# Experts in plain float32: weights stationary in two column tiles for gate and up, tokens in four for down

## The reference

```python
def swiglu(h, wg, wu, wd):
    g = jnp.einsum('btd,df->btf', h, wg)
    u = jnp.einsum('btd,df->btf', h, wu)
    return jnp.einsum('btf,fd->btd', jax.nn.silu(g) * u, wd)

def moe(h, router, wg, wu, wd):
    logits = jnp.einsum('btd,de->bte', h, router).astype(jnp.float32)
    vals, idx = lax.top_k(logits, TOP_K)
    gates = jax.nn.softmax(vals, axis=-1)
    comb = jnp.sum(jax.nn.one_hot(idx, N_EXPERTS, dtype=jnp.float32) * gates[..., None], axis=-2)
    out = jnp.zeros_like(h)
    for e in range(N_EXPERTS):
        out = out + comb[..., e:e + 1].astype(h.dtype) * swiglu(h, wg[e], wu[e], wd[e])
    return out
```

## Time and profile before

| what | value |
|---|---|
| median of 3 runs | 1280.8 us (1280.49 to 1281.12) |
| span of the profiled execution, first to last instruction | 1280.1 us |
| TensorE busy | 1262.4 us (99%), 6937 matmuls |
| VectorE, ScalarE busy | 934.3 us (73%), 803.0 us (63%) |
| HBM read | 340.57 MB, 273 GB/s over the span |
| granted clock of TensorE, mean | 0.999 |

### The profile page before, as it was taken

How to read it: one execution, slowest core, us unless ns; L and a number is a source line. 1 busy time by engine, 2 the same in 40 slices (tenths; PEclk the granted TensorE clock), 3 DMA queues, 4 the chain that set the end, 5 groups by cost and what they waited for, 6 DMA issues and landing times.

```text
span 1280.1 us, 18558 instructions
## 1 busy us (share of the span) xinstructions
PE 1262.4 (99%) x6937; PEld 1026.7 (80%) x6937; DVE 934.3 (73%) x888; ACT 803.0 (63%) x813; POOL 159.1 (12%) x175
## 2 busy tenths in 40 slices
PE   7999999999999999999999999999999999999998
PEld 5476699999974656788888888888888888888886
DVE  1667544443425667888888988988988988988897
ACT  2566533333324655767867877867867867777674
POOL 4131000000001020100310300400400400300300
PEclk9999999999999999999999999999999999999999
DMA  8261375445050624999999999999999999999994
GB/s 288 42 168 34 113 250 166 164 148 181 9 186 1 133 93 160 338 359 365 376 392 356 392 386 356 394 377 374 381 382 371 385 381 357 394 374 371 387 389 170
DMA packets 124595, 350.24 MB, mean 274 GB/s; under 512 B 8401, under 2 KB 33841, under 8 KB 124545
## 3 DMA queue, kind: packets, MB, share of 16 engines
q1 hardware_dynamic: 118896, 335.55, 71.9%
q0 software_dynamic: 4096, 12.43, 3.3%
q10 hardware_dynamic: 1552, 1.56, 0.4%
HBM read 340.57 MB, written 8.95 MB: 273 GB/s over the span
## 4 chain that ended last, share of the span: by engine, by line
PE 93%; DVE 3%; DMA 2%; ACT 1%; SPq 1%; issue 0%; DVEq 0%; ACTq 0%
PE ps L2337 38%; PE ps L2357 18%; PE ps L2244 11%; PE ps L1988 8%; PE ps L2260 5%; DMA ring<-in_w_in 2%; PE ps L2345 2%; PE ps L2061 1%; PE ps L2069 1%; PE ps L2121 1%; PE ps L2136 1%; PE ps L2174 1%; PE ps L2184 1%; PE ps L2001 1%; PE ps L2416 1%; PE ps L2085 1%
## 5 line engine op out<-in xcount | busy, mean ns | idle before, releaser
L1324 DVE TENSOR_TENSOR w_lo<-ring,w_hi 128x2048 fp32r<-128x2048 f32 (+1 forms) x322 | 675.2, 2124 | 178.8 <-ACT w_hi L938 176.4
L938 ACT ACTIVATE w_hi<-ring 128x2048 fp32r<-128x2048 f32 (+1 forms) x322 | 567.3, 1781 | 212.0 <-PE ps L2357 63.3
L2337 PE MATMUL ps<-w_hi,xg_hi 128*128 128x512 f32 (+1 forms) x768 | 287.8, 375 | 0.0
L2337 PE MATMUL ps<-w_hi,xg_lo 128*128 128x512 f32 (+1 forms) x768 | 286.1, 373 | 0.0
L2337 PE MATMUL ps<-w_lo,xg_hi 128*128 128x512 f32 (+1 forms) x768 | 285.4, 372 | 0.0
L2337 PEld LDWEIGHTS ps<-w_hi,xg_hi 128*128 128x128 f32 x768 | 144.6, 188 | 25.7
L2337 PEld LDWEIGHTS ps<-w_lo,xg_hi 128*128 128x128 f32 x768 | 144.2, 188 | 25.8
L2337 PEld LDWEIGHTS ps<-w_hi,xg_lo 128*128 128x128 f32 x768 | 144.6, 188 | 24.9
L2357 PE MATMUL ps<-w_hi,am_hi 128*128 128x512 f32 x340 | 133.7, 393 | 0.0
L2357 PE MATMUL ps<-w_lo,am_hi 128*128 128x512 f32 x340 | 132.5, 390 | 0.0
L2357 PE MATMUL ps<-w_hi,am_lo 128*128 128x512 f32 x340 | 132.3, 389 | 0.0
(11 more groups left out here) (357 smaller groups left out, 1435.2 us busy)
## 6 DMA issues: line engine op xcount, KB each, us to landing
ring<-in_moe_w_down SPq DMA_DIRECT2D x80, 1024.0 KB, 8.1
ring<-in_moe_w_gate SPq DMA_DIRECT2D x64, 1024.0 KB, 9.1
ring<-in_moe_w_up SPq DMA_DIRECT2D x64, 1024.0 KB, 9.4
ring<-in_moe_w_gate SPq DMA_DIRECT2D x32, 768.0 KB, 7.5
ring<-in_moe_w_up SPq DMA_DIRECT2D x32, 768.0 KB, 5.2
ring<-in_ffn_w_gate SPq DMA_DIRECT2D x11, 1024.0 KB, 7.4
ring<-in_ffn_w_up SPq DMA_DIRECT2D x11, 1024.0 KB, 5.3
ring<-in_ffn_w_down SPq DMA_DIRECT2D x10, 1024.0 KB, 5.2
```

The costliest lines, as they stand in the source:

```text
L938: A(hi[:, 0:size], src[:, 0:size], ACT.Copy).then_inc(hi_ready, 1)
L1324: V.tensor_tensor(lo[:, 0:size], src[:, 0:size], hi[:, 0:size].bitcast(F32), ALU.subtract).then_inc(lo_ready, 1)
L2337: ins = mm_(ps[:, b + c0 // 512, 0:c1 - c0], (xg_hi, xg_lo)[xp][:, k, :], w[wp][:, k % 2, c0:c1], start=(k == 0 and n == 0), stop=(k == KD ...
```

## The change

The experts leave float32r and the two parts. Weights are read as plain float32 from where the DMA put them.

- An expert has 96 places (`SLOTS`), three times 32.
- Gate and up: 64 columns of the weight are stationary, and the 96 tokens of `xg` move. Two column tiles take the two halves of a 128-column block, so the result stands with D_FF on the partitions, as down needs it; the transposes of `turn_chunk` and the split into `am_hi` and `am_lo` go.
- Down: the 96 tokens stand as three column tiles of 32 which move the first 768 columns of the weight; the fourth tile takes, one after another, the same three groups of tokens for the last 256 columns (`D_TAIL`). Their results stand on partitions 96 to 127 and are moved by ScalarE (`y_tail`).
- The ring of weights has twelve slots (`MOE_RING`): six in `ring`, six (`ring_more`) where `w_hi` and `w_lo` stood. A slot is free when TensorE has used it (`unit_used`).
- Gather of the first expert: both parts of a row accumulate in one bank and are turned once.
- Waits: up of chunk c + 1 waits for `act_done` of chunk c, `turn_rows` for `table_out`; at the head of the expert part `xh` waits for `stored`.

```diff
-SLOTS = P
+GRAN = DEC
+MAIN = P // GRAN - 1
+SLOTS = MAIN * GRAN
...
+BLOCKS = [w // P for w in WIDTH]
+HALF = P // 2
+D_TAIL = D // (MAIN + 1)
+D_LANE = D - D_TAIL
...
-DENSE_PAIRS, MOE_PAIRS = 3, 4
+DENSE_PAIRS = 3
+MOE_RING = 12
...
-        w_hi = [at(f"w_hi{i}", PHASE + 2 * SLOT_W * i, [P, SLOT_W], F32R) for i in range(MOE_PAIRS)]
-        w_lo = [at(f"w_lo{i}", PHASE + 2 * SLOT_W * i + SLOT_W, [P, SLOT_W], F32R) for i in range(MOE_PAIRS)]
+        w_hi = [at(f"w_hi{i}", PHASE + 2 * SLOT_W * i, [P, SLOT_W], F32R) for i in range(DENSE_PAIRS)]
+        w_lo = [at(f"w_lo{i}", PHASE + 2 * SLOT_W * i + SLOT_W, [P, SLOT_W], F32R) for i in range(DENSE_PAIRS)]
+        ring_more = [at(f"ring_more{i}", PHASE + SLOT_W * i, [P, SLOT_W]) for i in range(MOE_RING - RING)]
...
+        def unit_at(u):
+
+            i = u % MOE_RING
+            return ring[:, (MOE_AT + i) % RING, :] if i < RING else ring_more[i - RING][:, :]
...
-                sp.dma_start(ring[:, s, 0:n * wd].rearrange("p (n w) -> p n w", n=n), src).then_inc(w_ready[s], 16)
-
-            for u in range(RING):
-                slot_room(last_in_slot[(MOE_AT + u) % RING])
+                sp.dma_start(unit_at(u)[:, 0:n * wd].rearrange("p (n w) -> p n w", n=n), src).then_inc(unit_in[u % MOE_RING], 16)
+
+            for u in range(MOE_RING):
+                if u < RING:
+                    slot_room(last_in_slot[(MOE_AT + u) % RING])
+                elif u == RING:
+                    wait_full(sp, ("o", 1, len(GROUPS) - 1))
+                    sp.wait_ge(stored, 16 * DEPTH * 10)
                 load_unit(u, 0)
 
             def load_expert(j, e, first=0):
 
                 for u in range(first, len(EXPERT)):
-                    sp.wait_ge(lo_ready, j * len(EXPERT) + (ND + u - RING + 1))
+                    sp.wait_ge(unit_used, j * len(EXPERT) + (u - MOE_RING + 1))
...
-                    A(sgm[:, 0:WIDTH[c]], wide(0)[:, 0:WIDTH[c]], ACT.Silu).then_inc(silu_done, 1)
-
-                def chunk_high(c):
-                    w = WIDTH[c] // P
-                    act.wait_ge(aT_full, j * CHUNKS + (c + 1))
-                    A(am_hi[:, c % 2, 0:w, :], wide(4)[:, 0:w * P].rearrange("p (k c) -> p k c", k=w), ACT.Copy).then_inc(aT_high, 1)
+                    A(sgm[:, 0:BLOCKS[c], :], blocks(0, c), ACT.Silu).then_inc(silu_done, 1)
 
                 def output():
+
                     act.wait_ge(row_moved, j + 1)
-                    act.wait_ge(y_full, j + 1)
-                    A(y_out[:, :], wide(6), ACT.Copy, scale=slot_gate[:, 0:1]).then_inc(y_taken, 1)
+                    act.wait_ge(unit_used, j * len(EXPERT) + len(EXPERT))
+                    for g in range(MAIN):
+                        ins = A(y_out[GRAN * g:GRAN * g + GRAN, D_LANE:D], wide(6)[SLOTS:P, D_TAIL * g:D_TAIL * g + D_TAIL], ACT.Copy)
+                    ins.then_inc(y_tail, 1)
+                    A(y_out[0:SLOTS, 0:D_LANE], wide(6)[0:SLOTS, 0:D_LANE], ACT.Copy, scale=slot_gate[0:SLOTS, 0:1])
+                    act.wait_ge(y_tail, j + 1)
+                    A(y_out[0:SLOTS, D_LANE:D], y_out[0:SLOTS, D_LANE:D], ACT.Copy, scale=slot_gate[0:SLOTS, 0:1]).then_inc(y_taken, 1)
...
+                    V.tensor_tensor(am[:, c % 2, 0:BLOCKS[c], :], sgm[:, 0:BLOCKS[c], :], blocks(2, c), ALU.mult).then_inc(act_done, 1)
+
+                if not final:
+                    picks(bass.ds(j + 1, 1))
+                activations(0)
+                if not final:
+                    dve.wait_ge(row_moved, j + 1)
+                    table(j + 2)
+                activations(1)
+                activations(2)
+                if not final:
+                    dve.wait_ge(xgT_full, j + 2)
+                    tokens_second_half(5)
...
+                def lanes(b, x, w, main, tail, first, last):
+
+                    for c0 in range(0, main, 512):
+                        c1 = min(c0 + 512, main)
+                        for g in range(MAIN):
+                            ins = mm_(ps[GRAN * g:GRAN * g + GRAN, b + c0 // 512, 0:c1 - c0], x[:, GRAN * g:GRAN * g + GRAN], w[:, c0:c1],
+                                      start=first, stop=last)
+                        for g in range(MAIN):
+                            at_ = tail * g
+                            if c0 <= at_ < c1:
+                                ins = mm_(ps[SLOTS:P, b + c0 // 512, at_ - c0:at_ - c0 + tail], x[:, GRAN * g:GRAN * g + GRAN],
+                                          w[:, main:main + tail], start=(first and at_ == c0),
+                                          stop=(last and (g == MAIN - 1 or at_ + tail >= c1)))
+                    return ins
 
                 def project(kind, c, h):
+
                     u, wd = unit[kind, c, h], WIDTH[c]
+                    wait_unit(u)
+                    w = unit_at(u)[:, 0:2 * wd].rearrange("p (k c) -> p k c", k=2)
                     b = 0 if kind == "gate" else 2
-                    wait_unit(u)
-                    w = [x[u % MOE_PAIRS][:, 0:2 * wd].rearrange("p (k c) -> p k c", k=2) for x in (w_hi, w_lo)]
                     for k in (2 * h, 2 * h + 1):
-                        for c0 in range(0, wd, 512):
-                            c1 = min(c0 + 512, wd)
-                            for n, (wp, xp) in enumerate(PARTS):
-                                ins = mm_(ps[:, b + c0 // 512, 0:c1 - c0], (xg_hi, xg_lo)[xp][:, k, :], w[wp][:, k % 2, c0:c1],
-                                          start=(k == 0 and n == 0), stop=(k == KD - 1 and n == 2))
-                    in_use(ins, u)
-
-                def turn_chunk(c):
+                        for n in range(BLOCKS[c]):
+                            for half in range(2):
+                                c0 = P * n + HALF * half
+                                ins = mm_(ps[HALF * half:HALF * half + HALF, b + n // 4, P * (n % 4):P * (n % 4) + SLOTS], w[:, k % 2, c0:c0 + HALF],
+                                          xg[:, k, :], start=(k == 0 and n % 4 == 0), stop=(k == KD - 1 and n in (3, BLOCKS[c] - 1)))
+                    ins.then_inc(unit_used, 1)
...
+                        ins = lanes(6, am[:, c % 2, k0 + k, :], w[:, k, :], D_LANE, D_TAIL, c == 0 and h == 0 and k == 0, u == len(EXPERT) - 1 and k == n - 1)
+                    ins.then_inc(unit_used, 1)
...
-                project("gate", 1, 0)
-                project("gate", 1, 1)
-                if not final:
-                    pe.wait_ge(table_out, j + 2)
-                turn_chunk(0)
-                project("gate", 1, 2)
-                project("gate", 1, 3)
+                for h in range(4):
+                    project("gate", 1, h)
+                wait_turned(0)
                 for h in range(4):
                     project("up", 1, h)
-                pe.wait_ge(aT_out, j * CHUNKS + 1)
                 pe.wait_ge(y_taken, j + 1)
                 for h in range(4):
                     down(0, h)
                 pe.wait_ge(silu_done, j * CHUNKS + 2)
-                project("gate", 2, 0)
-                project("gate", 2, 1)
-                turn_chunk(1)
-                project("gate", 2, 2)
-                project("gate", 2, 3)
+                for h in range(4):
+                    project("gate", 2, h)
+                wait_turned(1)
                 for h in range(4):
                     project("up", 2, h)
-                pe.wait_ge(aT_out, j * CHUNKS + 2)
                 if not final:
+                    pe.wait_ge(table_out, j + 2)
                     turn_rows(j + 2)
-                down(1, 0)
-                down(1, 1)
-                if not final:
-                    pe.wait_ge(xg_ready, 2 * j + 4)
-                turn_chunk(2)
-                down(1, 2)
-                down(1, 3)
-                pe.wait_ge(aT_out, j * CHUNKS + 3)
+                for h in range(4):
+                    down(1, h)
+                wait_turned(2)
```

More of the change, by code:

```diff
@@ L200, in expert_plan @@
     return order + [("down", c, h) for c in (1, 2) for h in range(4)]
-def moe_events():
-    at = {key: u for u, key in enumerate(expert_plan())}
-    ev = {}
-    def put(key, what, c=0):
-        ev.setdefault(at[key] + MOE_PAIRS, []).append((what, c))
-    put(("gate", 0, 1), "picks")
-    for c in range(CHUNKS):
-        put(("gate", c, 3), "silu", c)
-        put(("up", c, 3), "act", c)
-    put(("up", 0, 3), "table")
-    put(("gate", 1, 1), "turned", 0)
-    put(("gate", 2, 1), "turned", 1)
-    put(("up", 2, 3), "tokens")
-    put(("down", 1, 1), "turned", 2)
-    put(("down", 2, 3), "output")
-    return ev
 def ffn_jobs():
@@ L442, in build @@
         w_ready = [sem(f"w_ready{i}") for i in range(RING)]
+        unit_in = [sem(f"unit_in{i}") for i in range(MOE_RING)]
+        unit_used = sem("unit_used")
         small_full = [sem(f"small_full{i}") for i in range(3)]
@@ L1284, in expert @@
[L1284 to L1298 removed]
+                    act.wait_ge(y_half, 1)
@@ L2303, in _ @@
                 c = slice(512 * half, 512 * half + 512)
```

(8 more changed lines are left out.)

264 lines of the change are left out of this document (93 added, 171 removed), and 8 rows, old and new, of tables (ACT_ORDER, DVE_ORDER).

## The result

The changed kernel takes 1306.2 us (median of 4 runs, 1304.9 to 1307.9) against 1280.6 for the kernel before on the same chip: ratio 1.0202, 95% interval 1.0187 to 1.0216. It is slower; the forecast was 1257 and the range ended at 1296. The profiled span is 1306.1 us.

A forecast was written before the change was run, and what follows sets the result against it. The prediction took TensorE's matmul stream as the bound. Seven periods gave -18.9 us, the last expert -5.1, head and tail +0.7: total -23.3, a span of 1256.8, forecast 1257 us, range 1235 to 1296.

The forecast's parts named there:

- held code: Rival in TensorE's expert loop: code is held or its fetch covered, period 89.1 us, total time 1240 us; chance 0.17.
- The step that was costed at 0.166 us and feared at 0.229: Gate and up: 352 steps an expert at 0.166 us, 58.4 us; at 0.229 a slow front end makes it 80.6.
- The slow front end: Rival at TensorE's issue and weight loads: 0.057 us a record, period 113.8 us, total time 1435 us; chance 0.15.
- the code of TensorE: Term for fetching the 242 KB expert loop: if not held, a miss each turn, taken as 2.5 us, period 91.6.
- The bound of 7.9: Upper bound for a code miss at a loop turn: 7.9 us, the median time to landing of a weight transfer.
- the prediction's turning point: Late code at loop turns: decides from a miss of 5.9 us on; at 7.9 the time is 1295 us, chance 0.10.
- the last part of the prediction: Profile signs expected afterwards; a long idle spell at each turn, with the clock falling behind it, would speak for late code.
- if every packet were as late, 5 us per packet would be short as well: Remark on late code: fifteen packets follow each turn's first, one per 5 us, short if all came 7.9 us late.
- 0, if it is held or the queued matmuls cover it: Lower bound for a code miss at a loop turn: 0 us, with code held or queued matmuls covering the fetch.
- Added waits: New waits before up and down, on tokens, table, ring slots and stores: all covered, 0 us.
- The DMA was no bound: Rival on weight transfers: if 377 GB/s is the limit, the period stays 93.9 us, total about 1275 us; chance 0.08.
- some 100 more packets: Sign expected in the profile after: some 100 more packets of code in queue 8.

The follow-up runs named there:

- the pause of 5.6 us: Kernel before with 14 reads of a word into a register at the end of each of TensorE's seven looped experts; 1337.5 us, 1.0442.
- the twelfth experiment: Changed kernel, TensorE's experts written out, pairs of down's units spread inside gate and up, plus a skipped loop for a second round; 1269.7 us, 0.9913.
- the half-loaded kernel: Changed kernel with TensorE's experts written out, loading only half of each weight unit's columns after the first expert; 1240.0 us.
- the interleaved kernel: Changed kernel with TensorE's experts written out and down's units put two by two between gate units of the next chunk; 1264.9 us, 0.9878.
- the first experiment: Changed kernel with a hint that TensorE's expert loop goes back; ratio 1.0111 to the kernel before.
- the half-loaded loop: Changed kernel, loop kept, loading only half of each weight unit's columns after the first expert; 1273.1 us.

## Why the prediction was wrong

**The reading of the kernel before held.** TensorE and the DMA both look full in the expert part; with 0.0 us of idle time before the matmuls of gate, up and down it is TensorE that bound it, and the changed kernel's TensorE stream is what the forecast said: 88.75 us an expert without code stalls (forecast 89.1), 1240.0 us for the run (forecast 1240 for held code; that these agree to the microsecond is luck, as the run has 3.5 us of stalls, against a period shorter by 0.35 us and a head and tail better than forecast). The step that was costed at 0.166 us and feared at 0.229 shows as 128 records in 5.50 us, of which the last runs its own 0.25: 127 intervals of 0.0413 us, 0.165 a step. A slice of down takes 1.29 us, as said. The slow front end did not appear: the records here start 41 ns apart.

**The step that failed** is the one called the code of TensorE. It named the mechanism (242 KB not held, a miss at each turn) and took 2.5 us for a miss at seven turns (the loop goes back six times), so 17 us for the run. That the loop would not be held rested on no row of the kernel before; the 94 packets from 610 to 1190 us show it. No run shows the 2.5 us. The runs show 66 us (1306.2 - 1240.0), in four parts:

- The miss: 6.1 us in the sequencer and 4.6 us of idle TensorE. 2.5 was made from the transfer time of a packet. The bound of 7.9, a transfer's time to landing, was the nearer row, for what was wanted was the time to landing of a packet, not its transfer time. Even so the miss alone did not decide: at six misses of 4.6 the time would be 1268, and the prediction's turning point was 5.9.
- The clock behind it, named in the last part of the prediction and left out of its sum. At the first turn the matmuls resume at 614.8, the full clock at 624.0, with 1.2 us idle between: (9.2 - 1.2)/2 = 4.0 us, as 49 records in 4.25 us against 2.28 agree for the first half. Over the six turns it is 21 us (TensorE works 42.5 us at the lower level). Here gaps of 4.5 to 4.7 us brought 10.2 us at the lower level five times and 6.8 once; the pause of 5.6 us brought 6.8, and the gap of 4.7 us in the twelfth experiment 3.4. What sets the length is open. Some 2 of the 4.0 us fall in the first page, and as the second page comes 5.7 us after the branch at either clock, at full clock the second gap would be longer by as much.
- The second page, 1.2 to 1.4 us at each turn, as it comes 5.7 to 6.0 us after the end of the branch.
- Pages late in sequence, 9.1 us in 17 stalls (28.5 in 41 where the loop is written out). The prediction said that fifteen packets follow, one per 5 us, and dismissed lateness there with "if every packet were as late, 5 us per packet would be short as well". That was the condition, and it was nearly met: 6.2 us against 5.3 to 5.5 in gate and up.

The parts add up. Idle by "issue" is 44.3 us in 29 stalls; as the listed idle time starts at the modelled end of a matmul, each stall is some 0.17 us longer from start to start: 49. The clock adds 21. Less the 4.5 of the half-loaded kernel (3.5 in 6 stalls) that is 66; the two spans differ by 1306.1 - 1238.1 = 68.0, so 2 us are not accounted for.

**Cover.** "0, if it is held or the queued matmuls cover it" stood among the bounds; what was missed is that the change itself removes the cover. Records of 0.07 us in down leave 1.3 us in TensorE's queue, where the kernel before had some 4.

**The rest.** Added waits cost 0, as said. The head is 2.8 us earlier than before (516.4 against 519.2), where -0.3 was forecast; the tail is as long as before to 0.3 us, where +1.0 was. The DMA was no bound at 358 GB/s; by the interleaved kernel it carries 385. The forecast of "some 100 more packets" met 117, but that row alone could not tell a cheap miss from a dear one. The loop of the kernel before, 61 KB, went back in 0.2 us with no packet fetched in six turns, and the 242 KB of the changed one were fetched anew at each; how much more than 61 KB would be held, no run shows.

## What to carry to other kernels

A change that trades long matmuls for many short ones is also a change of code: count the bytes of the loop body, the matmul time still queued when the loop closes, and the time that one packet of code keeps the engine busy against the time that it takes to come (here 5.4 against 6.2 us). Where a body can't be held, straight code with the slow and fast stretches mixed was worth 41 us of 1306 here. And price an idle gap with the clock behind it: here 4.6 us cost another 3.5 on average.

## What was unexpected

- A taken branch to code that is not held took 6.1 us beside full transfers and still 4.8 beside half of them; forward and back cost the same (6162 ns forward). The page after the target's came 5.7 to 6.0 us later still.
- A hint made the branch short (0.36 us) but not the pages behind it; with the head at the start of a block the branch took 2.5 us.
- TensorE's granted clock fell to 0.50 of full speed for 3.4 us after idle spells as short as 2.3 us (four of five such gaps in the first experiment) and stayed full after one of 3.4 us (the first turn of the half-loaded loop); it can fall while the engine still stands idle. Every stretch seen in the experts was 3.4, 6.8 or 10.2 us long.
- Two column tiles of 64, with 96 columns moving, started one record every 0.0413 us over 128 records, with the DMA at full traffic beside it.
